# The end of the Mamba mixer: group norms, first output weights and output products in another order

## What is computed

```python
def finish(y, xs, z):
    y = (y + d_skip * xs).reshape(b, L, SSM_INNER)           # 32 heads of 64, in 8 groups
    y = y * jax.nn.silu(z)
    yg = y.reshape(b, L, SSM_GROUPS, SSM_INNER // SSM_GROUPS)
    yg = yg * lax.rsqrt(jnp.mean(yg * yg, axis=-1, keepdims=True) + EPS)
    return (yg.reshape(b, L, SSM_INNER) * norm_w) @ out_w    # (256, 2048) @ (2048, 1024)
h = h + mod[:, :, 5] * y
```

## Time and profile before

| | us |
|---|---|
| median of three runs | 1999.91 |
| their range | 1997.24 to 2001.07 |
| the profiled execution, whole | 2001.32 |
| its span, first to last instruction | 1998.7 |
| mean granted clock of TensorE in it | 0.996 of full speed |

### The profile page before, as it was taken

How to read it: one execution, slowest core, us unless ns; L and a number is a source line. 1 busy time by engine, 2 the same in 40 slices (tenths; PEclk the granted TensorE clock), 3 DMA queues, 4 the chain that set the end, 5 groups by cost and what they waited for, 6 DMA issues and landing times. The chain is left out here.

```text
span 1998.7 us, 24597 instructions
## 1 busy us (share of the span) xinstructions
PE 1954.4 (98%) x9953; PEld 1630.0 (82%) x9953; DVE 1287.8 (64%) x1797; ACT 715.8 (36%) x1007; POOL 212.2 (11%) x151
## 2 busy tenths in 40 slices
PE   7999999999999999999999999999999998999998
PEld 4788888878888878888888888888888896688897
DVE  5755546678788575554767555566776578857654
ACT  4522222242311332223224222232444546735542
POOL 1000000100065200000110000001000004530001
PEclk9999999999999999999999999999999999999999
DMA  9544335543440254442654444355443445755554
GB/s 364 204 151 147 131 109 177 169 146 111 169 163 1 85 190 135 160 143 70 206 161 162 162 140 136 113 166 173 138 148 116 131 145 177 209 169 169 190 160 136
DMA packets 279302, 306.46 MB, mean 153 GB/s; under 512 B 9459, under 2 KB 249748, under 8 KB 277398
## 3 DMA queue, kind: packets, MB, share of 16 engines
q1 hardware_dynamic: 275398, 293.57, 46.3%
q10 hardware_dynamic: 3792, 11.33, 1.5%
HBM read 298.44 MB, written 6.43 MB: 153 GB/s over the span
## 5 line engine op out<-in xcount | busy, mean ns | idle before, releaser
L1775 PE MATMUL banks<-xhl,wh 128*128 128x512 f32 (+1 forms) x1756 | 664.9, 379 | 6.8 <-DVE xhl L1144 2.4
L1777 PE MATMUL banks<-xhl,wl 128*128 128x512 f32 (+1 forms) x1756 | 662.2, 377 | 0.0
L1776 PE MATMUL banks<-xhl,wh 128*128 128x512 f32 (+1 forms) x1756 | 662.1, 377 | 0.0
L1064 DVE TENSOR_TENSOR wl<-raw,wh 128x2048 fp32r<-128x2048 f32 (+2 forms) x193 | 398.7, 2066 | 236.2 <-ACT wh L626 230.9
L626 ACT ACTIVATE wh<-raw 128x2048 fp32r<-128x2048 f32 (+1 forms) x200 | 347.3, 1736 | 538.1 <-PE banks L1777 474.8
L1775 PEld LDWEIGHTS banks<-xhl,wh 128*128 128x128 f32 x1756 | 331.1, 189 | 75.2 <-DVE xhl L1144 6.5
L1777 PEld LDWEIGHTS banks<-xhl,wl 128*128 128x128 f32 x1756 | 330.9, 188 | 61.3
L1776 PEld LDWEIGHTS banks<-xhl,wh 128*128 128x128 f32 x1756 | 331.0, 188 | 59.3
L1775 PE MATMUL banks<-gh,wh 128*128 128x512 f32 (+1 forms) x704 | 255.4, 363 | 3.1 <-DVE wl L1064 3.1
L1776 PE MATMUL banks<-gl,wh 128*128 128x512 f32 (+1 forms) x704 | 255.2, 362 | 0.0
L1777 PE MATMUL banks<-gh,wl 128*128 128x512 f32 (+1 forms) x704 | 255.2, 362 | 0.0
(11 more groups left out here) (281 smaller groups left out, 2064.7 us busy)
## 6 DMA issues: line engine op xcount, KB each, us to landing
raw<-in_ffn_in SPq DMA_DIRECT2D x88, 1024.0 KB, 5.1
raw<-in_ffn_out SPq DMA_DIRECT2D x64, 704.0 KB, 4.6
ada_rawf<-in_ada_rest SPq DMA_DIRECT2D x60, 512.0 KB, 3.4
ada_rawo<-in_ada_rest SPq DMA_DIRECT2D x48, 512.0 KB, 3.3
raw<-in_mb_in_w SPq DMA_DIRECT2D x24, 1024.0 KB, 5.4
raw<-in_hy_in_w SPq DMA_DIRECT2D x12, 1024.0 KB, 5.1
afb<-decays SPq DMA_DIRECT2D x32, 256.0 KB, 4.3
raw<-in_mb_out_w SPq DMA_DIRECT2D x8, 1024.0 KB, 6.1
```

Source lines behind the costliest of these rows:

```text
L1064: dve.tensor_tensor(wl[n_slot][:, 0:cols], raw[r_slot][:, 0:cols], wh[n_slot][:, 0:cols].bitcast(F32), ALU.subtract).then_inc(w_lo, 1)
L1775: pe.matmul(dst, h, x_hi, start=start, stop=False)
L1776: pe.matmul(dst, h, x_lo, start=False, stop=False)
L1777: return pe.matmul(dst, l_, x_hi, start=False, stop=stop)
```

## The change

Nothing is computed differently; the same values are made at other moments, by partly other engines, in partly other memory. In words:

- SP loads chunk 0 of the output weights within the heads, behind the decay rows of head 8, instead of behind those of head 31.
- ACT makes chunk 0's high part in four pieces of 512 columns, behind the exponentials of heads 26, 28, 29 and 30.
- Sums of group 6 move from behind the last head into group 7, ahead of its last two heads' products. Group 7's sums go to `bank[7]`.
- The Sqrt is split: groups 0 to 6 at once, behind the last exponentials, and group 7 between the high parts of groups 0 and 1. The Sqrt that only fetched ACT's table is gone. The reciprocal is split likewise: that of groups 0 to 6 before the gating of the last group.
- DVE makes chunk 0's low part, into a tile of its own (`mwl`), before the gating of the last group instead of behind it. Chunk 1's high part goes to a tile of its own too (`mwh1`, where the C values lay) and is made before the square of the last group.
- PE spreads groups 0 to 5 before it sums group 7, and groups 6 and 7 behind the products of group 0.
- DVE makes `ynl` of group 0; POOL makes the other seven.
- DVE makes the low parts of chunks 1 and 2 right behind the last `normed`, without waiting for POOL's last `ynl`.

The diff, cut to its core:

```diff
@@ SP
+                if h == 2 * HPG:
+                    begin(MBOUT)
+                    sp.wait_ge(st_mm, GROUPS)
+                    load(MBOUT.raw, mbo_v[:, :, 0:P], 16, P)
-            begin(MBOUT)
-            for j in range(DT):
+            for j in range(1, DT):
                 sp.wait_ge(w_lo, MBOUT.w - 1 + j)
@@ ACT
             for h in range(1, HEADS):
                 exponentials(h)
-            act.activation(rs[:, 24:25], eps[:], ACT.Sqrt)
-            act.wait_ge(raw_in[MBOUT.raw % 2], 16 * (MBOUT.raw // 2 + 1))
-            act.activation(mwh[:], raw[MBOUT.raw % 2][:], ACT.Copy).then_inc(w_hi, 1)
+                if h in (26, 28, 29, 30):
+                    part = (26, 28, 29, 30).index(h)
+                    cols = slice(512 * part, 512 * part + 512)
+                    if part == 0:
+                        act.wait_ge(raw_in[MBOUT.raw % 2], 16 * (MBOUT.raw // 2 + 1))
+                    ins = act.activation(mwh[:, cols], first_raw[:, cols], ACT.Copy)
+            ins.then_inc(w_hi, 1)
+            group_roots(0, GROUPS - 1)
+            act.wait_ge(cs_done, HEADS)
+            act.wait_ge(cb_out, GROUPS)
+            act.wait_ge(raw_in[(MBOUT.raw + 1) % 2], 16 * ((MBOUT.raw + 1) // 2 + 1))
+            act.activation(mwh1[:], raw[(MBOUT.raw + 1) % 2][:], ACT.Copy).then_inc(w_hi, 1)
             square_y(GROUPS)
-            act.wait_ge(g_sum, GROUPS)
-            act.activation(rs[:, 0:2 * GROUPS], bank[0][:, 0:2 * GROUPS], ACT.Sqrt, bias=eps[:, 0:1],
-                           scale=1.0 / L).then_inc(g_rms, 1)
-            act.wait_ge(head_mm, HEADS)
-            r = MBOUT.raw + 1
-            split_hi(MBOUT.w + 1, CW, r % 2, r // 2 + 1, None)
             for g in range(GROUPS):
                 act.wait_ge(p_ready, MBN.q + g + 1)
                 act.activation(ynh[:, 2 * g:2 * g + 2, :].rearrange("p a n -> p (a n)"), ppn[g % 4][:],
                                ACT.Copy).then_inc(p_hi, 1)
+                if g == 0:
+                    group_roots(GROUPS - 1, GROUPS)
@@ DVE
+            dve.wait_ge(w_hi, MBOUT.w + 1)
+            dve.tensor_tensor(mwl[:], raw[MBOUT.raw % 2][:], mwh[:].bitcast(F32), ALU.subtract).then_inc(w_lo, 1)
+            group_inverses(0, GROUPS - 1)
             gate_y(GROUPS)
-            dve.wait_ge(w_hi, MBOUT.w + 1)
-            r = MBOUT.raw % 2
-            dve.tensor_tensor(wl[MBOUT.w % 2][:], raw[r][:], mwh[:].bitcast(F32), ALU.subtract).then_inc(w_lo, 1)
-            dve.wait_ge(g_rms, 1)
-            dve.reciprocal(rs[:, 0:2 * GROUPS], rs[:, 0:2 * GROUPS]).then_inc(g_rec, 1)
-            for g in range(GROUPS):
+            normed(0)
+            normed(1)
+            dve.wait_ge(p_hi, MBN.q + 1)
+            dve.tensor_tensor(ynl[:, 0:2, :].rearrange("p a n -> p (a n)"), ppn[0][:],
+                              ynh[:, 0:2, :].rearrange("p a n -> p (a n)").bitcast(F32), ALU.subtract).then_inc(p_lo, 1)
+            group_inverses(GROUPS - 1, GROUPS)
+            for g in range(2, GROUPS):
                 normed(g)
+            dve.wait_ge(w_hi, MBOUT.w + 2)
+            dve.tensor_tensor(wl[(MBOUT.w + 1) % 2][:], raw[(MBOUT.raw + 1) % 2][:], mwh1[:].bitcast(F32),
+                              ALU.subtract).then_inc(w_lo, 1)
+            chunk_lo(MBOUT, 2)
             dve.wait_ge(p_lo, MBN.q + GROUPS)
-            chunk_lo(MBOUT, 1)
@@ POOL
-            for g in range(GROUPS):
+            pool.wait_ge(p_lo, MBN.q + 1)
+            for g in range(1, GROUPS):
                 pool.wait_ge(p_hi, MBN.q + g + 1)
@@ PE, in the loop over the pairs of heads
+                    if g == GROUPS - 1 and p:
+                        sum_squares(GROUPS - 2)
                     pe.wait_ge(m_done, g * HPG + 2 * p + 2)
@@ PE, behind the heads
-            sum_squares(GROUPS - 2)
+            for g in range(GROUPS - 2):
+                spread(g)
             sum_squares(GROUPS - 1)
-            for g in range(GROUPS):
-                spread(g)
             for g in range(GROUPS):
                 pe.wait_ge(p_lo, MBN.q + g + 1)
                 ins = first_two(g)
+                if g == 0:
+                    spread(GROUPS - 2)
+                    spread(GROUPS - 1)
```

More of the change, by code:

```diff
@@ L1026, in _, with group_roots @@
             state_out(GROUPS - 1)
+            first_raw = raw[MBOUT.raw % 2]
             for h in range(1, HEADS):
                 exponentials(h)
-            act.activation(rs[:, 24:25], eps[:], ACT.Sqrt)
-            act.wait_ge(raw_in[MBOUT.raw % 2], 16 * (MBOUT.raw // 2 + 1))
-            act.activation(mwh[:], raw[MBOUT.raw % 2][:], ACT.Copy).then_inc(w_hi, 1)
-            square_y(GROUPS)
-            act.wait_ge(g_sum, GROUPS)
-            act.activation(rs[:, 0:2 * GROUPS], bank[0][:, 0:2 * GROUPS], ACT.Sqrt, bias=eps[:, 0:1],
-                           scale=1.0 / L).then_inc(g_rms, 1)
-            act.wait_ge(head_mm, HEADS)
-            r = MBOUT.raw + 1
-            split_hi(MBOUT.w + 1, CW, r % 2, r // 2 + 1, None)
+                if h in (26, 28, 29, 30):
[5 more added lines that the diff above has]
+            ins.then_inc(w_hi, 1)
+            def group_roots(g0, g1):
+                act.wait_ge(g_sum, g1)
+                act.activation(rs[:, 2 * g0:2 * g1], group_sums(g0)[:, 2 * g0:2 * g1], ACT.Sqrt, bias=eps[:, 0:1],
+                               scale=1.0 / L).then_inc(g_rms, 1)
+            group_roots(0, GROUPS - 1)
[3 more added lines that the diff above has]
+            act.activation(mwh1[:], raw[(MBOUT.raw + 1) % 2][:], ACT.Copy).then_inc(w_hi, 1)
+            square_y(GROUPS)
             for g in range(GROUPS):
@@ L2209, in sum_squares @@
                     for T in range(2):
-                        ins = pe.matmul(bank[0][:, 2 * g + T:2 * g + T + 1],
+                        ins = pe.matmul(group_sums(g)[:, 2 * g + T:2 * g + T + 1],
                                         tt[2 + (g + 1) % 2][:, mt * L + T * P:mt * L + T * P + P], ones[:, 0:1],
-                                        start=g + mt + T == 0, stop=g == GROUPS - 1 and mt + T == 2)
+                                        start=g in (0, GROUPS - 1) and mt + T == 0,
+                                        stop=g >= GROUPS - 2 and mt + T == 2)
                 ins.then_inc(g_sum, 1)
```

17 lines of the change are left out of this document (11 added, 6 removed).

## The result

| | before | after |
|---|---|---|
| median of the comparison, us | 1998.69 (22 runs) | 2002.04 (22 runs) |
| lowest and highest | 1995.72, 2001.07 | 1997.62, 2005.17 |
| ratio after/before | | 1.0015, 95% interval 1.0009 to 1.0021 |
| the profiled execution, span / whole | 1998.7 / 2001.32 | 2002.3 / 2004.11 |
| mean granted clock of the executions | 0.9951 (130, beside the experiments) | 0.9933 (22) |

The changed kernel is slower by 0.15%, about 3.0 us by the ratio (3.35 between the two medians). The forecast was 1.0 us faster, with 2001.9 as the upper end of the range; the median lies just outside. The difference is smaller than the 0.2% that the forecast counted as no change, but with 22 runs on each side its interval lies wholly above 1.

The account below looks back on a forecast made before the run. PE, busy 98% of the span, was taken as the bound, with chunk 3's start setting the end. A 1.36 us gain there less 0.4 for the load gave -0.96 us: 1998.9 us, range 1996.0 to 2001.9.

Parts of the forecast that it names:

- the sum moved ahead of the last head: Group 6's sum on PE now lies in front of the last head's end and delays it by 0.95 us.
- the hidden steps: Before the last gating: chunk 0's low part and the first reciprocal fit DVE's idle time and cost nothing.
- The first group: Behind the last head: PE starts group 0 at 1739.1 instead of 1741.99, 2.9 us earlier.
- The group 7 chain: Behind the spreads: group 7's sum and Sqrt, then group 1's high part and POOL's low part; cost 0.
- the turns: At chunks 1 and 2, DVE's splits and POOL's low parts alternate by whole instructions, spending the 2.9 us won; chance 63%.
- no turns: Rival at the splits: DVE and POOL run beside each other, chunk 3 starts 5.5 us earlier, 1994.8 us; chance 4%.
- POOL first: Rival at the splits: POOL keeps its run of low parts together, gain 2.1 us, 1997.8 us; chance 15%.
- the load among the heads: Chunk 0's load makes decay rows of heads 9 to 11 late: 0.4 us, bounds 0 to 3.3; net loss chance 18%.
- SP's own issue: Among the heads: SP issuing rows 2 us later, needed besides late rows for a loss over 0.2%; chance 3%.
- the pitch of the groups: PE's products behind the last head: 0.12 us per matmul, so 1.2 us per group.
- PE's clock might fall in them: In PE's new gaps between groups: a falling granted clock would make the prediction wrong; no size or chance given.

Follow-up runs that it names:

- e1_load4: Changed kernel with chunk 0's load issued behind head 4's decay rows instead of head 8's; ratio 1.0010 to the kernel before.
- f2_best: Changed kernel, load behind head 4's rows, DVE waiting for POOL between the splits of chunks 1 and 2, unread matmuls in PE's one gap; ratio 0.9993 to before.
- f3_halves: Changed kernel, load behind head 4's rows, DVE waiting for POOL between the two splits, chunk 1's split cut in halves; 1995.28 us, ratio 0.9984 to before.
- a2_fill: Changed kernel with 14 unread matmuls in each of PE's two gaps, in front of groups 5 and 6; ratio 0.9994 to the kernel before.
- c1_halves: Changed kernel with DVE's splits of chunks 1 and 2 each cut into two instructions of 1024 columns; ratio 0.9991 to the kernel before.
- a1_before: The kernel before, unchanged, run again as a control with a second trace; ratio 0.9996 to itself.
- e2_load4_fill: Changed kernel with chunk 0's load behind head 4's rows and 14 unread matmuls in each of PE's two gaps; ratio 0.9997 to the kernel before.
- c0_after: The changed kernel, unchanged, run again as a control with a second trace; ratio 1.0013 to the kernel before.
- a4_wait_second: Changed kernel with DVE waiting for POOL's last low part between the splits of chunks 1 and 2; ratio 0.9992 to the kernel before.
- g1_fill_one: Changed kernel with 14 unread matmuls in PE's first gap only, in front of group 5; ratio 1.0008 to the kernel before.
- f1_both: Changed kernel with chunk 0's load behind head 4's rows and DVE waiting for POOL between the splits of chunks 1 and 2; ratio 0.9987 to before.

## Why the prediction was wrong

**Right, the sum moved ahead of the last head.** Forecast +0.95 us. With the load out of the way (`e1_load4`, `f2_best`, `f3_halves`) the heads are 76.2 us, against 75.1 to 75.6 without the change: 0.8 on average, ACT's last piece included, of which the distance between DVE's products of heads 30 and 31 shows 0.13 (1.05 us instead of 0.93).

**Right, the hidden steps.** Chunk 0's low part and the first reciprocal end at 1735.8, and the gating behind them waits 0.94 us for PE, not for them. DVE's low part of group 0 took the 0.69 us that was taken from the gating's row. The first group is 3.1 us behind the head's end as the prediction counts it (1736.66 to 1739.74), forecast 3.1. The group 7 chain costs nothing that is seen.

**Right, the turns.** Forecast and measured: split of chunk 1 lengthened by about 0.4 (2.51 against 2.29, so 0.2), split of chunk 2 by 1.1 (3.19, so 0.9), POOL's last low part 16.5 us behind the head's end (16.3), two gaps of about 2 us on PE (1.82 and 1.81), no gap in front of chunk 3. In the kernel whose clock stays up, `a2_fill`, chunk 3 starts 25.8 us behind the table's point, which is 25.4 behind the head's end; the forecast had 1761.46 - 1736.03 = 25.4. Such a close hit is in part luck, as single steps were off by 0.2 us. Both rivals on this step, no turns and POOL first, are thereby out. (The -5.5 us that the prediction gives for the sum without turns leaves out its own 0.4; with it, it is -5.1, as in the rival's 1994.8.) The Trainium skill, page "SBUF — State Buffer", section "Who interferes with whom", has the port that VectorE and GpSimd share as an exclusive lock. By that rule, the trace agrees, and `c1_halves` shows what follows from it for a kernel: the lock is held for an instruction, so a shorter instruction gives it back sooner.

**Mis-sized, the load among the heads.** The term was 0.4 us, near a load of median length. The load took 9.0 us, the slow end of the earlier trace rows, and the cost was 1.0 to 1.1 us. The bounds of 0 to 3.3 held. The prediction itself said that the load would compete with rows in flight, and still stayed near the median. It also looked at the wrong row: the late one was head 9's, the next behind the load, and not head 10's. Head 9's row had 2.7 us to spare in the kernel before (landed 1683.83, used by ACT at 1686.52) and landed 3.7 us later in the changed one. SP's own issue, which the prediction named only for a loss of over 0.2%, had a part in it: it took 3.46 us instead of 0.3.

**The step that failed: the pitch of the groups.** Every matmul behind the gaps was counted at 0.12 us, the pitch at the full clock. The two gaps had been worked out, with their length, and that PE's clock might fall in them was named as a thing that would make the forecast wrong; it was not made a rival with a price. The stretch taken as evidence against it was 8.19 busy of 10 us with gaps of 0.49 and 1.32 us, not a gap of 1.8 us twice. Its price could have been estimated beforehand, from the number of matmuls behind the gaps: about 2 us for two groups at half the clock. What the runs show in place of 0.12 is 0.213 us a matmul for groups 6 and 7, 2.0 us on the path (`a2_fill`). It was what separated a gain of 1 from a loss. The Trainium skill, page "TensorE: Matmul & The Clock Gate", section "Part 1: The HAM clock gate (the "warmup" mystery)", says that the array's clock follows how busy PE has been of late, and knows two levels. By that, the trace agrees (1.00 and then 6.8 us at half). That alone was a reason to give this rival a chance, though not to say how large; `a1_before`, whose clock fell in a stretch where that of the same kernel had stayed up, shows that no single trace settles it.

**The account.** Of 4.0 us between forecast (-1.0) and result (+3.0), the fall on the path is 2.0 (27.8 against 25.8 in `a2_fill`) and the load 0.7 (1.1 instead of 0.4). Some 1.3 us remain, about as much as the ratio's interval reaches to either side. They may lie behind the stage: from the start of chunk 7 to the end the traces range from 209.2 to 212.7 us in the old order and from 210.5 to 215.1 in the new one, with falls of the clock of their own. One of 3.4 us, at 1926 to 1931, stands in 4 of the 12 traces with the new order (that of the changed kernel among them) and in none of the 5 with the old; it came without a fall in the stage too (`e2_load4_fill`), so it does not hang on that one. Ten of the twelve kernels with the new order have timed ratios above what their stage alone would give (their own falls within the heads taken off), and over all twelve the surplus is about 1 us in the mean. What causes that was not tried, and no cause is claimed.

## What to carry to other kernels

Where PE is the bound, ask of every edit what it does to PE's gaps, not only to its finish: behind two new gaps of 1.8 us the clock fell and took more than the 1.4 us that the new order had won, and it was enough to halve them by cutting DVE's instruction, or to fill them with dead work. Where DVE and POOL both work on SBUF operands, a long DVE instruction sets the wait of every short POOL one behind it; cut it, or keep the wait, where POOL feeds PE. A 1 MB load put among rows that are due soon is to be placed where the rows before it are nearly through: four heads earlier in none of five traces did DVE wait for the rows next behind it.

## What the runs showed of the hardware

- PE's granted clock went to 1.2 GHz in 3 of 3 traces with two gaps of 1.8 us in the changed order, for 6.8 us, each time before the second gap was over (which was 1.5 us in `c0_after`); with one such gap in two of three traces (`a4_wait_second`, `g1_fill_one`, not `f1_both`), for 3.4 us; with gaps of 0.77 us or 0.16 us in none. With two gaps of 1.84 us in the old order it was 3.4 us, with 1.51 none. In one of the five traces of the old order (`a1_before`) it fell for 6.8 us ahead of the groups, behind gaps of 0.50 and 0.65 us that the other four have as well.
- In every trace the clock falls in some more places (about 579, 1067 and 1433 us in both profiled ones), and some vary from execution to execution: at 1670 in 5 of the 12 traces with the new order and none of the 5 with the old, though in three of these five nothing is changed ahead of it. Whether that is chance is open.
- DVE and POOL alternate by whole instructions when both have more queued. A pair of POOL's 512-column low parts took 2.55 us alone, 3.5 beside one half split (1024 columns) and 4.5 beside one whole split or two halves.
- The first issue of a 256 KB row by SP behind a 1 MB load took 2.4 to 3.5 us of SP's time in the eight traces with the load behind head 8, and 0.32 in the five with it behind head 4. Without a load in front most take 0.3 to 0.4.
